# HGRN2 / sparse attention / S5 decoder trunk on one core: low halves and sums of squares made by VectorE, the norm's mean subtracted in place

## The reference, cut to what matters

```
x <- LayerNorm(alpha * x + mixer(x)) ;  x <- LayerNorm(alpha * x + relu(x @ w1)**2 @ w2)
HGRN2: f = lb + (1-lb) sigmoid(fz); S_t = diag(f_t) S_{t-1} + k_t v_t^T; o_t = S_t^T q_t  (8 heads of 128)
DSA:   score = sum_h w_h relu(qi_h . kidx); top 128 keys of a query; softmax attention over them
S5:    h_t = A h_{t-1} + B u_t (complex, diagonal); y = C h + d x; GLU
LayerNorm(v) = (v - mean) * rsqrt(var + 1e-5) * g + b ;  everything in float32
```

## Time and profile before

| | |
|---|---|
| median of 3 runs | 3753.68 us (3748.42 to 3760.49) |
| profiled execution, span from first to last instruction | 3748.7 us |
| what lies around the span | no time of its own is given for the profiled execution; the median is 5 us above its span |
| TensorE busy | 3153.9 us, 84% |
| VectorE busy | 1876.3 us, 50% |
| GpSimd busy | 1489.6 us, 40% |
| ScalarE busy | 1120.3 us, 30% |
| mean granted TensorE clock | 0.878 of full speed |

### The profile page before, as it was taken

How to read it: one execution, slowest core, us unless ns; L and a number is a source line. 1 busy time by engine, 2 the same in 40 slices (tenths; PEclk the granted TensorE clock), 3 DMA queues, 4 the chain that set the end, 5 groups by cost and what they waited for, 6 DMA issues and landing times.

```text
span 3748.7 us, 56136 instructions
## 1 busy us (share of the span) xinstructions
PE 3153.9 (84%) x22360; PEld 2861.9 (76%) x22360; DVE 1876.3 (50%) x2586; ACT 1120.3 (30%) x1827; POOL 1489.6 (40%) x837
## 2 busy tenths in 40 slices
PE   7889689998799788999555667899998888689998
PEld 7888689998589578999511114799998888689997
DVE  4666654252170326233489996460615655754152
ACT  3433332223322223222223222331224433342222
POOL 4222263445233035344345555543443222254443
PEclk9888799999789679999767778999998887899999
DMA  3211122322424212222200000222222212122221
GB/s 113 69 58 58 35 81 85 94 84 68 100 80 155 94 52 79 84 90 84 71 3 1 0 0 12 79 90 84 90 84 72 65 57 58 41 79 85 90 84 68
DMA packets 104309, 260.23 MB, mean 69 GB/s; under 512 B 9587, under 2 KB 44915, under 8 KB 103763
## 3 DMA queue, kind: packets, MB, share of 16 engines
q1 hardware_dynamic: 56592, 206.10, 17.5%
q10 hardware_dynamic: 42434, 34.07, 3.3%
q0 software_dynamic: 5120, 17.83, 1.3%
HBM read 239.09 MB, written 18.88 MB: 69 GB/s over the span
## 4 chain that ended last, share of the span: by engine, by line
PE 65%; DVE 16%; issue 7%; ACT 6%; POOL 3%; DMA 1%; ACTq 1%; DVEq 0%; POOLq 0%; SPq 0%
PE lp L1476 18%; PE lp L1478 17%; PE lp L1477 17%; PE mb L1548 4%; DVE ph L1381 2%; DVE lw L1030 2%; DVE rot L1353 2%; POOL lw L474 1%; DVE lw L1027 1%; DVE dd L1096 1%; PE lp L1705 1%; DVE qt L994 1%; DVE lw L1362 1%; PE mb L1559 1%; PE mb L1648 1%
## 5 line engine op out<-in xcount | busy, mean ns | idle before, releaser
L350 POOL TENSOR_TENSOR wl<-raw,wh 128x1024 fp32r<-128x1024 f32 x389 | 959.6, 2468 | 1449.8 <-ACT wh L554 834.3
L1476 PE MATMUL lp<-xh,wh 128*128 128x260 f32 x4176 | 1238.7, 297 | 101.9 <-POOL xl L360 94.0
L1478 PE MATMUL lp<-xh,wl 128*128 128x260 f32 x4176 | 1212.4, 290 | 0.0
L1477 PE MATMUL lp<-xl,wh 128*128 128x260 f32 x4176 | 1210.8, 290 | 0.0
L1476 PEld LDWEIGHTS lp<-xh,wh 128*128 128x128 f32 x4176 | 823.6, 197 | 115.5 <-issue 79.3
L1477 PEld LDWEIGHTS lp<-xl,wh 128*128 128x128 f32 x4176 | 822.3, 197 | 0.5
L1478 PEld LDWEIGHTS lp<-xh,wl 128*128 128x128 f32 x4176 | 821.2, 197 | 0.0
L1476 PE MATMUL lp<-hh,wh 128*128 128x260 f32 x2048 | 589.1, 288 | 41.0 <-DVE hl L1450 41.0
L1478 PE MATMUL lp<-hh,wl 128*128 128x260 f32 x2048 | 587.6, 287 | 0.0
L1477 PE MATMUL lp<-hl,wh 128*128 128x260 f32 x2048 | 585.9, 286 | 0.0
L1476 PEld LDWEIGHTS lp<-hh,wh 128*128 128x128 f32 x2048 | 395.6, 193 | 42.6 <-POOL wl L350 42.6
(11 more groups left out here) (307 smaller groups left out, 3713.7 us busy)
## 6 DMA issues: line engine op xcount, KB each, us to landing
raw<-in_wstream SPq DMA_DIRECT2D x389, 512.0 KB, 3.5
s<-in_s_in ACTq DMA_DIRECT2D x16, 512.0 KB, 4.1
out_hg_s<-s ACTq DMA_DIRECT2D x16, 512.0 KB, 3.3
pg<-in_kpages POOLq DMA_DIRECT2D x16, 512.0 KB, 5.7
pg<-in_vpages POOLq DMA_DIRECT2D x16, 512.0 KB, 5.4
bias_rows<-bsm ACTq DMA_DIRECT2D x1, 2560.0 KB
x<-in_xT ACTq DMA_DIRECT2D x4, 520.0 KB, 7.9
out_kT<-r ACTq DMA_DIRECT2D x1, 2080.0 KB, 11.4
```

What stands on the lines that cost most here:

```text
L350: pool.tensor_tensor(wl[:, s, :], raw[:, r_, :], wh[:, s, :].bitcast(F32), ALU.subtract).then_inc(w_low, 1)
L1476: pe.matmul(bank(T, half), wh[:, slot, w], hi[:, k0 + k, t], start=first, stop=False)
L1477: pe.matmul(bank(T, half), wh[:, slot, w], lo[:, k0 + k, t], start=False, stop=False)
L1478: ins = pe.matmul(bank(T, half), wl[:, slot, w], hi[:, k0 + k, t], start=False, stop=last)
```

## The change

GpSimd keeps only the constants, the page loads of the attention and its share of the S5 recurrence. All `low` (389), `split` (all but 7 blocks of S5) and `square_sum` go to VectorE, as do `kp` and the scaling of `s`. The first `square_sum` of a norm is a copy, so the memset goes. In the norm the mean is subtracted in `r` itself, for three blocks while ScalarE makes `rstd`, and then three blocks ahead. The attention's page loads no longer stand between `low`s: index pages first, then all key and value pages.

```diff
@@ VectorE: the helpers, moved here from GpSimd @@
+        def low(n, s, r_):
+            dve.wait_ge(w_high, n + 1)
+            dve.tensor_tensor(wl[:, s, :], raw[:, r_, :], wh[:, s, :].bitcast(F32), ALU.subtract).then_inc(w_low, 1)
+        def split(src, n0, ms=range(KT)):
+            for m in ms:
+                dve.wait_ge(xh_ready, n0 + m + 1)
+                dve.tensor_tensor(xl[:, m, :], src[:, m, :], xh[:, m, :].bitcast(F32), ALU.subtract).then_inc(xl_ready, 1)
+        def square_sum(ln, m):
+            if m == KT - 1:
+                return
+            dve.wait_ge(sq_ready, 8 * ln + m + 1)
+            if m:
+                dve.wait_ge(sq_added, 7 * ln + m)
+                dve.tensor_tensor(rsq, rsq, lw[:, 2 + m % 2, :], ALU.add).then_inc(sq_added, 1)
+            else:
+                dve.tensor_copy(rsq, lw[:, 2, :]).then_inc(sq_added, 1)
@@ norm @@
+            for m in range(3):
+                center(m)                      # r[m] -= mean, in place
+            link.wait()
+            dve.wait_ge(var_ready, ln + 1)
+            dve.wait_ge(rstd_ready, ln + 1)
             for m in range(KT):
-                link.step(dve.tensor_tensor(lw[:, 6 + m % 2, :], r[:, m, :], mean, ALU.subtract))
-                dve.tensor_tensor(lw[:, 6 + m % 2, :], lw[:, 6 + m % 2, :], rstd, ALU.mult).then_inc(norm_ready, 1)
+                dve.tensor_tensor(lw[:, 6 + m % 2, :], r[:, m, :], rstd, ALU.mult).then_inc(norm_ready, 1)
+                center(m + 3)
+                if m:
+                    lows(m - 1)                # split(x, n0, (m - 1,))
+                link.wait()
+            lows(KT - 1)
@@ HGRN2, one head on VectorE @@
                         if l == 0:
                             dve.tensor_tensor(qe[:], q_[:, 0:NP_], lf[:, 0:NP_], ALU.mult).then_inc(qt_ready, 1)
+                            ahead(0)           # low of chunk 4 (h + 1) + 0 + AHEAD
+                        if l == 1:
+                            dve.tensor_tensor(kp[:], k_[:, 0:NP_], ee[:, 0, :], ALU.mult).then_inc(kp_ready, 1)
                         if l >= 2:
                             level(G, l - 1, k_, q_)
+                        if l == 3:
+                            ahead(1)
                     for l in range(3, LEVELS + 1):
                         merge(G, l)
+                        if l == 3:
+                            ahead(2)
+                        if l == 4:
+                            dve.tensor_tensor(s0b[:, G % 2], s0b[:, G % 2], fs, ALU.mult).then_inc(sf_ready, 1)
                     dve.tensor_tensor(mixA[:, h, :], ot, g_, ALU.mult).then_inc(mix_ready, 1)
+                    ahead(3)
@@ DSA: lows between the steps of the selection @@
-                    for _ in range(k // 8):
+                    for i in range(k // 8):
                         link.step(dve.max(top8[0:rows, :], a))
                         link.step(dve.match_replace(a, top8[0:rows, :], a, TAKEN))
+                        if i in lows:
+                            low_at(c0 + lows[i] + AHEAD)
@@ MLP, w1 and w2 @@
                     for c in range(4):
+                        low(i * 4 + n, n % SPL, n % RAW)   # n = y["cm"] + 32 * half + c + AHEAD
                         dve.wait_ge(tile_out, i * 4 + (t1 + c + 1))
                 for m in range(KT):
+                    low_at(c2 + 2 * m + AHEAD)
+                    low_at(c2 + 2 * m + 1 + AHEAD)
+                    if half and m:
+                        square_sum(ln + 1, m - 1)
                     residual(...)
```

More of the change, by code:

```diff
@@ L344, in _ @@
     def _(pool):
[L345 to L374, removed]
         pool.memset(ones_mean[:], 1.0 / D).then_inc(consts_set, 1)
@@ L441, in _ @@
                 pool.wait_ge(pt_loaded, 16)
[L442 removed]
+                pool.wait_ge(w_high, y["c"] + AHEAD + 1)
                 kv_pages(0)
                 kv_pages(1)
[L445 to L455 removed]
+                pool.wait_ge(w_high, y["c"] + AHEAD + 2)
+                for n in range(NS):
+                    index_pages(n)
+                for u in range(2, 2 * NS):
                     kv_pages(u)
[L457 to L458 removed]
             if y["kind"] == 2:
@@ L1038, in _ @@
         dve.tensor_tensor(lbp[:], lbp[:], lbt[:, 0:1, :].to_broadcast([P, DEPTH, KT]), ALU.subtract).then_inc(lb_ready, 1)
+        for n in range(AHEAD):
+            low_at(n)
+        split(x, 0)
         dve.wait_ge(lb_ready, 2)
@@ L1060, in _, with ahead @@
                 link.step(dve.tensor_copy(lmask[:].rearrange("p l t -> p (l t)"), masks32))
+                for j in range(4):
+                    low_at(c0 + j + AHEAD)
                 for h in range(HEADS):
+                    def ahead(j):
+                        if h < HEADS - 1:
+                            low_at(c0 + 4 * (h + 1) + j + AHEAD)
                     G, p = g0 + h, h % 2
@@ L1148, in _ @@
                 dve.tensor_tensor(kiT, kiT, kv_, ALU.mult).then_inc(ki_norm, 1)
+                for c in range(2, 5):
+                    low_at(c0 + c + AHEAD)
                 dve.wait_ge(wi_ready, 2)
@@ L1154, in _ @@
                                       ).then_inc(w3_ready, 1)
+                for c in range(5, 7):
+                    low_at(c0 + c + AHEAD)
                 for u, (qb, h) in enumerate(IUNITS):
@@ L1194, in _ @@
                                   ).then_inc(sprod, 1)
+                for c in range(21, 29):
+                    low_at(c0 + c + AHEAD)
                 dve.wait_ge(sy_ready, 1)
@@ L1442, in _ @@
                     for c in range(4):
+                        n = y["cm"] + 32 * half + c + AHEAD
+                        low(i * 4 + n, n % SPL, n % RAW)
                         dve.wait_ge(tile_out, i * 4 + (t1 + c + 1))
@@ L1453, in _ @@
                 dve.wait_ge(tile_out, t1 + HHALF)
+                c2 = y["cm"] + 32 * half + HHALF
                 for m in range(KT):
-                    residual(y["cm"] + 32 * half + HHALF + 2 * m + 1, t1 + HHALF + m, m, ("first", "second")[half])
-            norm(ln + 1, y)
+                    low_at(c2 + 2 * m + AHEAD)
+                    low_at(c2 + 2 * m + 1 + AHEAD)
+                    if half and m:
+                        square_sum(ln + 1, m - 1)
+                    residual(c2 + 2 * m + 1, t1 + HHALF + m, m, ("first", "second")[half])
+            norm(ln + 1, y, 8 * (3 * y["i"] + 3) if y["i"] < L - 1 else None)
     @block.tensor
```

129 lines of the change are left out of this document (43 added, 86 removed).

## The result

The changed kernel takes 3597.03 us (median of 4 runs, 3587.92 to 3613.37) against 3753.97 us: a ratio of 0.9585, 95% interval 0.9558 to 0.9613. The profiled execution has a span of 3592.3 us, 156.4 less than before (forecast: 142.5).

The account below looks back on a forecast made before the run. TensorE, busy 84% of 3748.7 us, was taken as the bound, gains coming only at its waits and low clock. Terms -64 - 23 - 16 - 15 - 20 - 9 - 3 + 5 + 2.5 = -142.5 gave 3611 us, range 3545 to 3675.

Parts of the forecast that it names:

- Stretching: VectorE's two-SBUF-operand instructions are held up until a GpSimd instruction ends; without it hl 0.70, dd 0.42, lows 1.2 us.
- Heads, start of the levels: 16 HGRN heads: level 1 starts net 4.0 us earlier per head, -64 us.
- Heads, clock: HGRN levels: shorter gap of some 3.3 us keeps TensorE's clock up in a quarter of cases, -23 us (bounds 0 and -92).
- the prediction's paragraph on them: HGRN heads: transposes do not count as busy for the clock gate, so the clock falls, with none of the 92 us.
- MLP: Between w1 and w2, 8 places: hl loses 1.98 us each, -16 us; clock stays up in two thirds, -15 us.
- Norms: Chunks behind 7 norms: last xl 3.3 us earlier, TensorE gains 2.9, -20 us; small stretches and first xl behind mixers, -3.
- GLU, start: GLU after S5: pairs of chunks take 11.5 us instead of 13.0, -9 us; start: third chunk's load delayed, +2.5 us.
- Attention: Selection: 10 lows on full VectorE make chunks 13, 14, 16 wait, +5 us; moving the page loads changes nothing.
- A: HGRN heads and MLP: clock falls in every shortened gap, and selection costs 15: -94, 3660 us; chance 0.25.
- B: HGRN heads and MLP: clock stays up everywhere: -220, 3534 us; chance 0.15.
- C: HGRN heads: VectorE's low waits for wh, and TensorE for kt behind that low: +98, 3852 us; chance 0.04.
- D: Stretching is VectorE's own, no gain comes; w1 chunks take VectorE 6.6 us against 5.74: +109, some 3860 us; chance 0.01.

Follow-up runs that it names:

- the kernels with useless work: Changed kernel plus a GpSimd subtraction, copy or memset of 1024 columns per chunk in HGRN heads and w1, result unread: 3649.45, 3641.12 and 3601.82 us.
- after: The changed kernel itself, against the kernel before: 3597.03 us, ratio 0.9585.
- stir_set: Changed kernel plus a useless GpSimd memset of 1024 columns for each chunk in the HGRN heads and w1 stretches: 3601.82 us, ratio 0.9609 to before.
- sel_pool: Changed kernel with the ten low halves among the attention's selection steps given back to GpSimd: 3603.74 us, ratio 0.9590 to before.
- fill_mlp: Changed kernel plus 24 useless matmuls of 256 columns between w1 and w2 in each of the 8 MLP halves: 3599.09 us.
- fill_norm: Changed kernel plus 48 useless matmuls of 128 columns behind each norm's statistics: 3611.05 us, ratio 0.9597 to before.
- pages_later: Changed kernel with GpSimd's page loads from the tenth pair on waiting until the last value tile is stored: 3585.30 us, ratio 0.9548 to before.
- low_later: Changed kernel with one low half per head moved later on VectorE, behind the level work of l = 6: 3633.06 us, ratio 0.9669 to before.
- fill_heads: Changed kernel plus 14 useless matmuls of 256 columns in TensorE's wait ahead of level 1 in HGRN heads: 3565.73 us, ratio 0.9489 to before.

## Why the prediction was right, and where it was not

The span came out 13.9 us below its forecast and the median 14. The heads gave 13 us more than forecast and the norms 8 us more, the MLP 9 us less, so part of the errors cancelled.

**Stretching.** Right, in cause and size: 0.70, 0.42 and 1.22 us for what I put at 0.70, 0.42 and 1.2; shown by the kernels with useless work. One reading was loose. I wrote that `hl` gains almost exactly one GpSimd low. It gains 1.98 us beside a low of 2.5, since the low has been running for 0.4 us when `hl` begins. The sum used the 1.98 and is not touched. And the condition of two operands is not the whole of it, as the cast `hh` shows.

**Heads, start of the levels.** Forecast 4.0 us a head, measured 14.44 - 10.10 = 4.34, -69.5 us for 16.

**Heads, clock.** Forecast -23, and -100.0 + 69.5 = -30.5 is left for it; this is a difference and not measured by itself. I gave it a quarter of the heads, and the gap 3.3 us. In the profiled execution the wait ahead of level 1 was 3.1 us in 5 heads and the clock fell behind it in all 5; it was 1.8 to 2.4 us in 9 heads and the clock fell there in 2. So it held in 7 of 14 gaps. The `kp` transposes stand ahead of the gap in every head, and the fall that the prediction's paragraph on them allowed for did not come in these seven. The same holds over six executions of kernels with equal heads (those named next): 40 waits of 3.1 us with a fall at each of them, and 44 waits of 1.8 to 2.4 us with a fall at 8. What decides which wait a head has was not worked out. The two sums came out near each other partly by chance: kernels whose heads are the same instruction for instruction on TensorE, VectorE and ScalarE (after, stir_set, sel_pool, fill_mlp, fill_norm, pages_later) have 632.7 to 668.4 us in the 14 intervals. That may also be why the changed kernel spreads by 25 us between runs where the kernel before had 12; the intervals of the other runs are not known.

**MLP.** The wait went from 5.1 to 3.2 us, -15.5 against -16 forecast. The clock's -15, for two thirds of the places, was the term that was mis-sized: about -6.6 is left for it. In the profiled execution the clock stays up in 2 of the 8 places, falls for 3.4 us in 2 and for 6.8 us in 4. These windows, a place where it held and one where it fell, show that the same 3.2 us wait goes either way; before it fell always:

```profile
559.10:562.40 3.30, 0.12 (x2) 0.03 (x1) 1.92 (x4) 1.55 (x2) 0.00 (x0) 1.00 0.38 150
562.40:568.20 5.80, 5.80 (x48) 5.80 (x49) 1.14 (x1) 0.00 (x0) 0.00 (x0) 1.00 0.28 90
1653.10:1659.90 6.80, 5.77 (x26) 5.78 (x27) 1.92 (x2) 0.00 (x0) 0.00 (x0) 0.50 0.24 80
```

**Norms.** Mis-sized, -20 and -3 against -30.8, 4.4 us a norm and not 2.9. In the first norm the last `xl` ends 18.6 us behind `mean` where it ended 22.95 before: 4.3 us earlier, not the 3.3 of the prediction. The first begins 0.6 us later than before, but is shorter and ends 0.2 us earlier, as forecast. VectorE's timeline there, the last two, and the last row of GpSimd's before, both with the mean's own start at 457.92 and 514.0:

```profile
474.28 0.70 DVE L871 TENSOR_TENSOR xl<-x,xh 128x520 fp32r<-128x520 f32 x1
475.84 0.70 DVE L871 TENSOR_TENSOR xl<-x,xh 128x520 fp32r<-128x520 f32 x1 [0.86 <-ACT xh L477]
```
```profile
534.26 2.69 POOL L360 TENSOR_TENSOR xl<-x,xh 128x520 fp32r<-128x520 f32 x2 [2.16 <-ACT xh L584]
```

**GLU, start.** -9.1 for -9 and +1.7 for +2.5. TensorE is busy in all 11.50 us of a pair:

```profile
2275.00:2286.50 11.50, 11.50 (x98) 11.50 (x98) 5.18 (x7) 3.82 (x5) 0.00 (x0) 1.00 0.29 93
```

**Attention.** +6.2 for +5, the right number by a wrong step, so by luck. The chunks that were to wait 1.5, 1.8 and 1.8 us wait 0.6 together. What costs 4.5 us is the sentence "Moving the attention's page loads changes nothing: they wait for used pages": they do, but they also stood behind GpSimd's lows, and without that cover one met a store on which ScalarE waited. The clock and the length of that store move this stage by as much: in nine other kernels with the changed order of loads it takes 481 to 490 us from norm to norm, for 485.7 in the changed kernel and 479.2 before.

**Rivals.** A (the clock falls in every shortened gap) and B (nowhere) were both refuted within one execution; the fall is decided place by place. C (a low waits for `wh` and TensorE for what stands behind the low) did not come: in the heads of the profiled execution the 28 lows of a layer wait 0.22 us for `wh` in all, and TensorE's one wait for a low is 0.6 us. In low_later a low in VectorE's queue does make TensorE wait in the levels, but by its own length and not by a wait for `wh`. D fell with the first row of `hl`.

## What to carry to other kernels

When an instruction on GpSimd reads SBUF, price it twice: its own time, and what is left of it again on a two-operand VectorE instruction that starts beside it. Look for a duration whose median is its minimum plus most of one GpSimd instruction (here 1.98 of 2.5 us). When a wait of TensorE is shortened, ask where it goes and what the clock does behind it: moving 1.1 us from ahead of the levels into them cost 36 us, and filling the waits with useless matmuls, together with the later page loads, gained 56. And when work leaves a queue, list the transfers that stood behind it: they start earlier, and may meet one that somebody waits for.

## What was not expected of the hardware

- VectorE holds GpSimd up as well: a GpSimd subtraction of 1.98 us took 7.68 beside two-operand VectorE instructions that followed each other without a gap.
- A memset on GpSimd, which reads nothing, left `hl` at 0.70 us, but a one-operand cast that began inside it took 1.08 to 1.24 us instead of 0.43.
- Behind a wait of 1.44 us amid small matmuls the clock fell from 1.00 to 0.50 in 8 of 9 heads of low_later, in the one shown for over 26 us with TensorE busy throughout; behind 3.2 us after dense matmuls it stayed up in 2 of 8 places.
- The length of a wait alone does not order the falls: the clock fell behind all six waits of 1.44 us in fill_heads, and behind 8 of 44 waits of 1.8 to 2.4 us.
- What brings the clock down in a head's last part, where TensorE has no wait, was not settled.
